# Samples' queries against their states: fp32 column tiles, two samples at a time, in place of split fp32r products

## Time and profile before

| what | value |
|---|---|
| median of the runs | 2483.55 us (2481.48 to 2484.72) |
| span of the profiled execution | 2482.3 us, core 0, mean granted clock 0.996 |
| TensorE matmuls busy | 2433.8 us, 98% of the span |
| VectorE busy | 1902.2 us, 77% |
| ScalarE busy | 1102.6 us, 44% |
| GpSimd busy | 277.6 us, 11% |
| chain that ended last | TensorE 89%, VectorE 5%, DMA 3%, issue 2%, ScalarE 1% |

### The profile page before, as it was taken

One profiled execution on the slowest core, in us unless ns is written; L12 is line 12 of the kernel. 1 busy time (PEld: TensorE's weight loads), 2 busy tenths in 40 slices (PEclk: granted clock), 3 DMA queues, 4 the chain that ended last, 5 costly groups with the idle time before them and its releaser, 6 DMA issues.

```text
span 2482.3 us, 44073 instructions
## 1 busy us (share of the span) xinstructions
PE 2433.8 (98%) x18106; PEld 2392.7 (96%) x18106; DVE 1902.2 (77%) x2813; ACT 1102.6 (44%) x1652; POOL 277.6 (11%) x474
## 2 busy tenths in 40 slices
PE   8999999999999999999999999999999999999996
PEld 7999999999899999999999999999999999998996
DVE  7558678685788788787787888876767778989775
ACT  6344445444534443443434344444445445445443
POOL 2002011020210000000000011100000110332111
PEclk9999999999999999999999999999999999999998
DMA  6325344353444334433443346653578668669455
GB/s 186 83 55 180 103 124 143 90 170 92 156 144 109 98 90 119 119 102 95 111 119 103 104 121 181 181 144 108 161 222 268 216 220 292 197 194 294 142 151 159
DMA packets 456249, 369.04 MB, mean 149 GB/s; under 512 B 15989, under 2 KB 425761, under 8 KB 453537
## 3 DMA queue, kind: packets, MB, share of 16 engines
q1 hardware_dynamic: 419826, 238.91, 34.9%
q0 software_dynamic: 36224, 127.32, 15.7%
HBM read 286.50 MB, written 79.68 MB: 148 GB/s over the span
## 4 chain that ended last, share of the span: by engine, by line
PE 89%; DVE 5%; DMA 3%; issue 2%; ACT 1%; POOL 0%; SPq 0%; ACTq 0%; DVEq 0%; POOLq 0%
PE bank L1826 35%; PE acc L1826 28%; PE acc L1685 18%; PE acc L1641 1%; DVE ring_lo L1944 1%; PE acc L1577 1%; PE bank L1610 1%; PE bank L1638 1%; DMA x_rows<-in_x_prompt 1%; PE bank L1635 1%; PE bank L1614 0%; DMA mix_tile<-ma_d 0%; DMA pa<-in_w_branch_a 0%; DMA x_f<-zw_d 0%; PE bank L1564 0%
## 5 line engine op out<-in xcount | busy, mean ns | idle before, releaser
L1944 DVE TENSOR_TENSOR ring_lo<-pa,ring_hi 128x1024 fp32r<-128x1024 f32 x532 | 649.6, 1221 | 202.3 <-ACT ring_hi L1078 198.8
L1078 ACT ACTIVATE ring_hi<-pa 128x1024 fp32r<-128x1024 f32 x532 | 561.6, 1056 | 374.3 <-PE bank L1826 224.8
L1685 PE MATMUL acc<-act_y,w_hi 128*128 128x288 f32 x2560 | 520.1, 298 | 0.0
L1826 PE MATMUL bank<-act_y,ring_hi 128*128 128x288 f32 x2432 | 478.4, 296 | 1.9 <-DMA act_y<-zs_d 1.2
L1826 PE MATMUL bank<-act_x,ring_hi 128*128 128x288 f32 x2432 | 475.8, 294 | 3.2 <-DMA act_x<-zp_d 1.7
L1826 PE MATMUL acc<-act_x,ring_hi 128*128 128x288 f32 x2176 | 435.3, 294 | 1.3 <-DVE ring_lo L1944 1.3
L1685 PEld LDWEIGHTS acc<-act_y,w_hi 128*128 128x128 f32 x2560 | 410.7, 189 | 3.7 <-issue 1.2
L1826 PEld LDWEIGHTS bank<-act_x,ring_hi 128*128 128x128 f32 x2432 | 387.5, 189 | 4.2 <-DMA act_x<-zp_d 2.0
L1826 PEld LDWEIGHTS bank<-act_y,ring_hi 128*128 128x128 f32 x2432 | 385.1, 189 | 3.1 <-DMA act_y<-zs_d 1.4
L1685 PE MATMUL acc<-act_y,w_lo 128*128 128x288 f32 x1280 | 377.9, 295 | 0.0
L1826 PEld LDWEIGHTS acc<-act_x,ring_hi 128*128 128x128 f32 x2176 | 351.2, 189 | 1.5 <-issue 1.5
(11 more groups left out here) (365 smaller groups left out, 2835.8 us busy)
## 6 DMA issues: line engine op xcount, KB each, us to landing
pa<-in_w_in SPq DMA_DIRECT2D x208, 512.0 KB, 5.3
raw<-in_w_in SPq DMA_DIRECT2D x40, 1024.0 KB, 5.6
states<-in_state_gla POOLq DMA_DIRECT2D x64, 256.0 KB, 3.0
out<-states POOLq DMA_DIRECT2D x64, 256.0 KB, 2.8
pa<-in_w_branch_a SPq DMA_DIRECT2D x32, 512.0 KB, 6.3
pa<-in_w_branch_b SPq DMA_DIRECT2D x32, 512.0 KB, 6.8
pa<-in_w_out SPq DMA_DIRECT2D x32, 512.0 KB, 6.7
zt_d<-gate_tile POOLq DMA_DIRECT2D x12, 576.0 KB, 3.5
```

Source lines behind the costliest of these rows:

```text
L1078: A(ring_hi[g % RING][:, :], piece_of[src][u % 2][:, :], ACT.Copy).then_inc(part_hi, 1)
L1685: mm = nc.tensor.matmul(half_bank[h % 2][:, 0:HALF], (w_hi, w_lo)[a][par][:, k * P:(k + 1) * P], y_of(k, b, j), start=(k == 0 and n == 0), ...
L1826: mm = nc.tensor.matmul(out, (ring_hi, ring_lo)[a][r][:, k * P:(k + 1) * P], slot_of(slot, b)[:, k, :], start=(p in (0, 1, 3) and k == 0 a ...
L1944: V.tensor_tensor(ring_lo[g % RING][:, :], piece_of[SOURCE[p]][u % 2][:, :], ring_hi[g % RING][:, :].bitcast(F32), ALU.subtract).then_inc( ...
```

## The change

The queries are no longer split, nor the states: they are multiplied in fp32. Samples 2a and 2a+1 are taken together, ahead of sample 2a. For sample b of the pair and key slice kk, 32 columns of queries (8 of them of the sample, the others zero or of other pairs' places) are the stationary operand and 512 state columns the moving one, and the result goes to the 32 rows of `b_smp` that begin at 32*(2b + kk). The four matmuls of a pair thus have four different groups of 32 output rows, that is, four column tiles of the array. `pair` adds the two key slices in place of the high and low queries. The states have four places (three in `states`, one where `s_hi` was), `q_state` moves to the space of `v2`, and the squares of the sample outputs to that of `kd_one`. ScalarE's `s_hi` and VectorE's `s_lo` are gone; `pad_queries` is done every second sample.

```diff
+SLOTS_S = 4
-        s_hi = nc.alloc_sbuf_tensor_at("s_hi", [P, KK, DV], F32R, offset=gate_at)
-        q_state = nc.alloc_sbuf_tensor_at("q_state", [P, DV], F32, offset=gate_at)
+        state_3 = nc.alloc_sbuf_tensor_at("state_3", [P, KK, DV], F32, offset=gate_at)
+        q_state = nc.alloc_sbuf_tensor_at("q_state", [P, DV], F32, offset=v2_at)
-        q_seq = put("q_seq", [P, KK, P], F32R)
+        q_pad = put("q_pad", [P, 2, KK, 2, TS // 2], F32)
-        states = put("states", [P, 2, KK, DV], F32)
-        s_lo = put("s_lo", [P, KK, DV], F32R)
+        states = put("states", [P, SLOTS_S - 1, KK, DV], F32)
+        sq_s = nc.alloc_sbuf_tensor_at("sq_s", [P, VV * TS], F32, offset=kd_one_at)
+        def state_of(j):
+            n = j % SLOTS_S
+            return states[:, n, :, :] if n < SLOTS_S - 1 else state_3[:, :, :]
...
             def load_state(i, j):
                 rows = state_gla[0, j, i, :, :].rearrange("(k p) v -> k p v", p=P)
+                if NS * i + j >= SLOTS_S:
+                    pool.wait_ge(st_out[j % SLOTS_S], KK * 16 * (NS // SLOTS_S * i + j // SLOTS_S))
                 for kk in range(KK):
-                    if NS * i + j >= 2:
-                        pool.wait_ge(st_out[j % 2][kk], 8 * NS * i + 16 * (j // 2))
-                    pool.dma_start(states[:, j % 2, kk, :], rows[kk]).then_inc(st_in[j % 2], 16)
-            load_state(0, 0)
-            load_state(0, 1)
+                    pool.dma_start(state_of(j)[:, kk, :], rows[kk]).then_inc(st_in[j // 2 % 2], 16)
+            for j in range(SLOTS_S - 1):
+                load_state(0, j)
             pool.wait_ge(c_out, 32)
+            load_state(0, SLOTS_S - 1)
             for h in range(NH):
...
                 i = head_at(h, 12)
                 if i:
-                    load_state(i, 0)
-                    load_state(i, 1)
+                    for j in range(SLOTS_S):
+                        load_state(i, j)
...
-                    if j + 2 < NS:
-                        load_state(i, j + 2)
+                    if j + SLOTS_S < NS:
+                        load_state(i, j + SLOTS_S)
...
-            def seq_round(i, j):
-                act.wait_ge(st_in[j % 2], KK * (i * (8 * NS) + 16 * (j // 2 + 1)))
-                if j:
+            def mask_keys(i, j):
+                if i + j:
                     act.wait_ge(seq_mm, i * NS + j)
-                elif i:
-                    act.wait_ge(chunk_mm, i * NCH)
-                A(s_hi[:, :, :], states[:, j % 2, :, :], ACT.Copy).then_inc(state_hi, 1)
+                if i and j == 0:
+                    act.wait_ge(mean_mm, i * NCH)
                 act.wait_ge(seq_kd, i + 1)
                 A(kd_one[:, :], kd_seq[:, j // (NS // 2), :].bitcast(F32), ACT.Copy, scale=seq_sel[:, j:j + 1]
                   ).then_inc(kd_hi, 1)
...
+            def pair_queries(i, a):
+                pe.wait_ge(q_set, i * (NS // 2) + a + 1)
+                if a == 0 and i:
+                    pe.wait_ge(inter_saved, i)
+                if a == 0 and i + 1 < H:
+                    pe.wait_ge(neg_part, i + 2)
+                    pe.wait_ge(abs_done, i + 2)
+                pe.wait_ge(st_in[a % 2], 2 * KK * 16 * (NS // SLOTS_S * i + a // 2 + 1))
+                for b in range(2):
+                    for kk in range(KK):
+                        r = (b * KK + kk) * (TS // 2)
+                        nc.tensor.matmul(b_smp[r:r + TS // 2, :], q_pad[:, a % 2, kk, b, :], state_of(2 * a + b)[:, kk, :],
+                                         start=(a == 0), stop=(a == NS // 2 - 1))
             def sample(i, j):
                 pe.wait_ge(kd_hi, i * NS + j + 1)
-                pe.wait_ge(seq_split, i * NS + j + 1)
...
-                for kk in range(KK):
-                    for n2, st in enumerate((s_hi, s_lo)):
-                        nc.tensor.matmul(b_smp, q_seq[:, kk, :], st[:, kk, :],
-                                         start=(j == 0 and kk == 0 and n2 == 0),
-                                         stop=(j == NS - 1 and kk == KK - 1 and n2 == 1))
...
                 i, j = bit_at(h, AT_SEQ)
                 if i is not None:
+                    if j % 2 == 0:
+                        pair_queries(i, j // 2)
                     sample(i, j)
...
-            def sample_split(i, j):
-                if j:
-                    dve.wait_ge(seq_mm, i * NS + j)
+            def pad_queries(i, a):
+                if a >= 2:
+                    dve.wait_ge(seq_mm, i * NS + 2 * (a - 2) + 1)
                 else:
                     dve.wait_ge(qe_ready, i + 1)
-                link(V.memset(q_seq[:, :, :].bitcast(F32), 0.0))
-                q_j = qe[:, :, TP + j * LS:TP + (j + 1) * LS]
-                link(V.tensor_copy(q_seq[:, :, j * LS:(j + 1) * LS], q_j))
-                V.tensor_tensor(q_seq[:, :, TS + j * LS:TS + (j + 1) * LS], q_j,
-                                q_seq[:, :, j * LS:(j + 1) * LS].bitcast(F32), ALU.subtract)
-                dve.wait_ge(state_hi, i * NS + j + 1)
-                V.tensor_tensor(s_lo[:, :, :], states[:, j % 2, :, :], s_hi[:, :, :].bitcast(F32),
-                                ALU.subtract).then_inc(seq_split, 1)
+                    if i:
+                        dve.wait_ge(seq_mm, i * NS)
+                link(V.memset(q_pad[:, a % 2, :, :, :], 0.0))
+                two = qe[:, :, TP + 2 * a * LS:TP + 2 * (a + 1) * LS].rearrange("p k (b c) -> p k b c", b=2)
+                V.tensor_copy(q_pad[:, a % 2, :, :, a * LS:(a + 1) * LS], two).then_inc(q_set, 1)
...
-                    sq = gate_tile[:, 1, 0:VV * TS].rearrange("p (v t) -> p v t", v=VV)
+                    sq = sq_s[:, :].rearrange("p (v t) -> p v t", v=VV)
...
-                ij = bit_at(h, AT_SEQ)
-                if ij[0] is not None:
-                    sample_split(*ij)
+                i, j = bit_at(h, AT_SEQ)
+                if i is not None and j % 2 == 0:
+                    pad_queries(i, j // 2)
```

More of the change, by code:

```diff
@@ L256, in hybrid_kernel @@
         kd_seq = put("kd_seq", [P, 2, DK], F32R)
-        q_seq = put("q_seq", [P, KK, P], F32R)
+        q_pad = put("q_pad", [P, 2, KK, 2, TS // 2], F32)
         assert cursor["at"] == g_at + 2 * QUARTER
-        states = put("states", [P, 2, KK, DV], F32)
-        s_lo = put("s_lo", [P, KK, DV], F32R)
+        states = put("states", [P, SLOTS_S - 1, KK, DV], F32)
         kd_rows = put("kd_rows", [P, NT, DK], F32)
+        kd_one_at = cursor["at"]
         kd_one = put("kd_one", [P, DK], F32R)
+        sq_s = nc.alloc_sbuf_tensor_at("sq_s", [P, VV * TS], F32, offset=kd_one_at)
+        assert VV * TS <= DK
         ssq = put("ssq", [P, P], F32)
@@ L338, in hybrid_kernel @@
         v2_hi, v2_ready = sem("v2_hi"), sem("v2_ready")
-        state_hi, seq_split = sem("state_hi"), sem("seq_split")
+        q_set = sem("q_set")
         key_hi, kd_hi, seq_kd, seq_mm, seq_upd = sem("key_hi"), sem("kd_hi"), sem("seq_kd"), sem("seq_mm"), sem("seq_upd")
-        st_in = [sem(f"st_in{n}") for n in range(2)]
-        st_out = [[sem(f"st_out{n}{k}") for k in range(2)] for n in range(2)]
+        st_in = [sem(f"st_in{n}") for n in range(SLOTS_S // 2)]
+        st_out = [sem(f"st_out{n}") for n in range(SLOTS_S)]
         inter_saved, chunk_mm, chunk_sq, chunk_state, sp_out = (
@@ L749, in _ @@
                         pool.wait_ge(seq_upd, (i * NS + j) * KK + kk + 1)
-                        pool.dma_start(rows[kk], states[:, j % 2, kk, :]).then_inc(st_out[j % 2][kk], 16)
-                    if j + 2 < NS:
-                        load_state(i, j + 2)
+                        pool.dma_start(rows[kk], state_of(j)[:, kk, :]).then_inc(st_out[j % SLOTS_S], 16)
+                    if j + SLOTS_S < NS:
+                        load_state(i, j + SLOTS_S)
                 i = head_at(h, AT_CHUNK[NT - 1] + 2)
@@ L769, in _ @@
             pool.dma_start(gate_d[0, GATE_UNITS - 1], mix_tile[:, 1, :]).then_inc(extra_out, 16)
-            for n in range(2):
-                for kk in range(KK):
-                    pool.wait_ge(st_out[n][kk], 16 * (NS // 2) * H)
+            for n in range(SLOTS_S):
+                pool.wait_ge(st_out[n], KK * 16 * (NS // SLOTS_S) * H)
             pool.wait_ge(sp_out, 16 * H)
@@ L1163, in seq_values @@
                 if i:
-                    act.wait_ge(seq_mm, i * NS)
+                    act.wait_ge(chunk_mm, i * NCH)
                 for g in range(2):
@@ L1251, in _ @@
                 if i is not None:
-                    seq_round(i, j)
+                    mask_keys(i, j)
                 i, l = bit_at(h, AT_LEVEL[:-1])
@@ L1864, in _ @@
             dve.wait_ge(ident_in, 16)
-            V.tensor_tensor(pair[:, :], ident[:, 0:TS], ident[:, TS:P], ALU.add)
+            of_rows = ident[:, :].rearrange("p (b k a c) -> p b k a c", b=2, k=KK, c=LS)
+            for b in range(2):
+                V.tensor_tensor(pair[:, :].rearrange("p (a b c) -> p a b c", b=2, c=LS)[:, :, b, :],
```

(24 more changed lines are left out.)

## The result

The changed kernel takes 2468.74 us (2468.57 to 2471.55 in four runs) against 2482.64 us beside it: a ratio of 0.9946, with a 95% interval of 0.9934 to 0.9958. That is 13.9 us faster. The forecast was no measurable change, 2487.6 us. The time lies inside the stated range, which reached down to rival A, and is 1.7 us above that rival's 2467 us; I had given it one chance in three.

The account below looks back on a forecast made before the run. TensorE's stream was taken to bound the kernel: span 2482.3, +8.0 for query products and shape change, -4.0 for waits, gives 2486.3; runs' median stands 1.25 above, so 2487.6 us. The range ran from about rival A's 2467 to 2500.

Parts of the forecast that it names:

- rival A: Query products: four column tiles run wholly side by side, 0.86 us a pair plus 0.19, so 2467 us; chance 0.33.
- The reading of what bounds the kernel: GLA stage: nearly a plain sum of TensorE's work, with VectorE and ScalarE as cover and few real waits.
- Added to TensorE: Fp32 query products: a pair's eight passes form a staircase of five steps of 0.43, 2.15 us a pair.
- The bounds: Query products of a pair: 3.44 us if passes run one after another, 0.86 if four tiles run side by side.
- The change of shape: TensorE going to a tiled array shape and back: 0.19 us once a pair, bounded by 0 and 0.43.
- The waits: TensorE's waits: four for the sum of squares (2.9 us) and one for masked keys (1.1) go, together -4.0 us.
- The moves priced at nothing: Moved state loads and new waits, such as `pair_queries` for both states of a pair, priced at 0.
- the fourfold reading: Query products: four column tiles suggest a fourfold overlap, which the forecast said splitting fp32 into two passes undoes.

Follow-up runs that it names:

- e1: Changed kernel with a pair's four query products all in one column tile, so they follow each other; 2509.37 us, ratio 1.0108.
- e6: Changed kernel without the query products of three pairs in four, only each head's first pair being multiplied; 2454.44 us.
- e7: Kernel before the change, with states and queries rounded and split only for each head's first sample; 2476.33 us, ratio 0.9974.
- e4: Changed kernel with each sample's two products ahead of its own increment, two tiles at a time in 32 groups; 2485.58 us, ratio 1.0013.
- e5: The changed kernel again, unaltered, beside the later experiments; 2468.19 us, ratio 0.9940.
- e2: Changed kernel with two column tiles a pair in place of four, issued in turn (tile 0, 1, 0, 1); 2480.49 us, ratio 0.9994.
- e3: Changed kernel with two column tiles a pair in place of four, issued in a row (tile 0, 0, 1, 1); 2481.79 us, ratio 0.9994.
- e8: Changed kernel with each head's first two pairs multiplied one behind the other ahead of sample 0; 2467.37 us, ratio 0.9939.

## Why the prediction was wrong

**The reading of what bounds the kernel was right.** The stage was a sum on TensorE, and every experiment moved by its own term of that sum.

**The step that failed** is in "Added to TensorE": "If that order holds across tiles, tile 1's first pass can't start before tile 0's second has". It doesn't hold. The rows from which I took the order were of matmuls over the whole array (128*128 in the earlier trace rows); with no column tiles in them, they could not show whether one tile's work overtakes another's, either way. The products took 0.86 us plus the step in, in place of 2.15. The step is worth 16 x (2.15 - 0.86) = 20.6 us, the whole way from the forecast of 2487.6 to 2467, which rival A had with the same remaining terms. From there 2.4 for the change of shape and 0.4 for waits, both below, lead to 2469.8, and the kernel before ran 0.9 faster beside the changed one (2482.64) than ahead of it (2483.55): 2468.9, against 2468.74.

**The bounds were right.** 3.44 and 0.86 a pair, from the 0.43 of a pass of L1641, are what e1 (3.55 with the step in) and the changed kernel (1.00) show. The high one was the bound for tiles that can't overlap.

**The change of shape was sized too low:** 0.19 a pair taken, 0.14 ahead (1.00 less 0.86) and 0.20 behind (0.66 less 0.46) measured. That is 0.15 a pair, 2.4 us. It was read from L1655, which works on 64 rows, with short passes of 64 columns. Behind a pair the next weights' load starts at 186.35, 0.52 after the last passes have started; without a pair ahead (e6) it starts together with the last pass. How the 0.34 follow from this I did not work out. It lay within its bounds of 0 and 0.43.

**The waits** were taken as -4.0. Without the splitting they are worth 5.2 (e7), and the changed kernel gets 3.6 of it: over the same stage its trace is 14.2 us shorter, of which 10.6 are the products. Most of the 1.6 that is missing comes back at one place in each of the first three heads (in the first, half 21), sample 3. There the product of the queries no longer stands between the half's matmuls and the mean, and the mean waits for ScalarE to save the half. The chain of the changed kernel:

```profile
211.38 6.34 PE acc L1699 x48
217.73 0.02 issue
217.75 0.03 ACT qk L1110
217.77 0.23 issue
218.00 0.23 ACT qk L1110
218.23 0.14 issue
218.36 0.46 PE acc L1679 x2
218.82 6.40 PE acc L1699 x48
```

7.44 us from one set of 48 to the next, where 6.34 + 0.46 + 0.22 = 7.02 would do without the wait: 0.42 a head, just the difference of 0.98 (e7) and 0.56. In e4, where sample 3 has its own products at this place, TensorE doesn't wait for ScalarE's `qk` at all. I had said that nothing but TensorE would be late next.

**The moves priced at nothing** cost nothing that shows: TensorE waits nowhere for a state's load or for the prepared queries. I did not test the loads by themselves.

**The rest of the 15.6 us of span** is mostly the run's. The 32 projection matmuls behind the transposes of x took 5.36 us before and 3.82 after:

```profile
37.85:43.21 5.36, 5.36 (x34) 5.36 (x34) 3.81 (x7) 0.42 (x2) 4.04 (x9) 0.68 0.45 107
```

```profile
38.17:41.99 3.82, 3.82 (x34) 3.82 (x34) 3.79 (x8) 0.42 (x2) 2.81 (x6) 1.00 0.34 89
```

The eighth column is the granted clock: 0.68 on average in one, 0.50 (1.2 GHz) from 38.20 to 41.55 and 2.4 GHz ahead of it and behind, and 1.00 in the other, behind the same transposes. The changed kernel profiled again (e5) shows 0.68 and 5.38. So these 1.5 us belong to the execution, not to the change. The changed kernel's trace has such a stretch elsewhere, in the second stage, from 2278 to 2282 us at 0.57 on average, where TensorE had just been idle for 1.40 us; its chain there, then that of e5 at the same place:

```profile
2278.55 4.86 PE acc L1842 x24
```

```profile
2280.22 3.40 PE acc L1842 x24
```

That is 1.5 us the other way. It is made up for by waits of that stage, above all one for a load of `act_x`: 1.7 us in the trace of before, 0.2 in this one, 0.4 in e5's.

In sum, by the first matmul of each stage: -1.2 ahead of the GLA stage (the 1.5, less 0.3 by which the transposes began later), -10.6 for the products with the change of shape and -5.2 + 1.6 for waits within it, -0.2 behind it; that is the whole of the 15.6. The -14.2 of the stage agree with the medians, which are 13.9 apart.

## What to carry to other kernels

A pass with 32 stationary columns took as long here as one with 128 (0.43 us): before pricing fp32 at its two passes, count how many such products can lie in different column tiles, since four side by side took 1.00 us and two took 0.98. The price of a group was that of its deepest tile plus 0.34 us for leaving and re-entering the full shape, so group as many independent products as the buffers allow, and don't mind their order (e2 and e3 differ by nothing). And a rule of order that was read from rows in which no other order could have shown is not evidence; keep both cases open, and give the better one its due.

## What the runs showed that I had not expected

- A matmul that waits for its own column tile held up none of another tile, neither with its second pass nor with a second matmul behind it (e3: both orders 1.84 to 1.85 us). The Trainium skill, "TensorE: Matmul & The Clock Gate", "The mechanism", has matmuls start and end strictly in program order and loads overlap only with other row groups; in e3 a later matmul starts first, and in the changed kernel four loads run under matmuls on the same rows. The measurements decide.
- Four fp32 column tiles, each fed with its own 512 columns of states, take two steps of some 0.43, as one tile's two passes would: 1.00 us for eight passes, 0.98 for four. No loss to the fourfold reading shows.
- The change of shape cost 0.12 to 0.14 us going in and 0.20 coming out, whether the group had 4, 8 or 16 passes (e4, the changed kernel, e8).
- The same matmuls behind the same transposes ran for 3.4 us at a granted clock of 0.50 in some executions (before, e5) and at 1.00 throughout in others (the changed kernel), 1.5 us apart.
